# A hybrid decoder layer: the first block's products interleaved with its transposes, and other PSUM banks and places for small work in the dense stage

## The reference

```
u = rmsnorm(h, norm_mix_g);  proj = u @ w_in            # 2824 columns: q, k, v, z, conv inputs, dt
oa = banded attention, window 128, with sinks (4 heads)  # per-head RMS norm of q and k
oc = three dilated attentions, windows 128/512/2048 (4 heads), joined by their softmax weights
ob = SSD scan over causal_dwconv(x, B, C), gated by silu(z)
h  = h + concat(oa, ob, oc) @ w_out
h  = h + square(relu(rmsnorm(h, norm_mlp_g) @ w_up)) @ w_down    # d_ff = 4096
```

## Time and profile before

| | |
|---|---|
| median of three runs | 2558.17 us |
| the profiled execution | 2557.03 us, of which its span is 2554.8 us |
| PE busy | 2410.4 us, 94% of the span |
| DVE, ACT, POOL busy | 1234.8, 846.2, 278.7 us |
| mean granted clock of TensorE | 0.98 of full |
| chain that ended last | PE 74%, DVE 6%, ACT 3%; PE core_dense L2299 alone 64% |

### The profile page before, as it was taken

One profiled execution on the slowest core, in us unless ns is written; L12 is line 12 of the kernel. 1 busy time (PEld: TensorE's weight loads), 2 busy tenths in 40 slices (PEclk: granted clock), 3 DMA queues, 4 the chain that ended last, 5 costly groups with the idle time before them and its releaser, 6 DMA issues.

```text
span 2554.8 us, 43225 instructions
## 1 busy us (share of the span) xinstructions
PE 2410.4 (94%) x17509; PEld 1411.2 (55%) x17509; DVE 1234.8 (48%) x2843; ACT 846.2 (33%) x1533; POOL 278.7 (11%) x305
## 2 busy tenths in 40 slices
PE   7899968999888999999899999989999999999999
PEld 4455535555434555444455554445655447788887
DVE  3445446566646767742644654135566521422222
ACT  4444235464435443331433331124432111311210
POOL 0111222111102211001110100011101001000000
PEclk8899989999999999999999999999999999999999
DMA  6454264665574667775434556533455553322232
GB/s 209 166 173 165 100 229 150 215 209 181 177 237 154 213 204 230 246 257 180 154 118 153 153 163 178 159 119 106 156 172 167 159 163 117 96 92 99 93 99 81
DMA packets 327588, 414.44 MB, mean 162 GB/s; under 512 B 62111, under 2 KB 248095, under 8 KB 327136
## 3 DMA queue, kind: packets, MB, share of 16 engines
q1 hardware_dynamic: 327392, 411.69, 50.0%
HBM read 300.00 MB, written 111.62 MB: 161 GB/s over the span
## 4 chain that ended last, share of the span: by engine, by line
PE 74%; DVE 6%; ACT 3%; issue 2%; DMA 1%; SPq 1%; POOL 0%; DVEq 0%; ACTq 0%; POOLq 0%
PE core_dense L2299 64%; PE core_spare L2399 2%; PE core_spare L2413 1%; PE core_spare L2387 1%; PE core_spare L2425 1%; PE core_spare L2553 1%; DVE core_col L2013 1%; DVE core_p L1939 1%; ACT core_p L1715 1%; PE core_spare L2547 1%; PE core_spare L2531 0%; PE core_spare L2539 0%; DVE core_h L1907 0%; PE core_spare L2533 0%; DVE core_r L1895 0%
## 5 line engine op out<-in xcount | busy, mean ns | idle before, releaser
L2299 PE MATMUL core_dense<-core_u,core_ring 128*128 128x512 f16 (+2 forms) x4800 | 870.2, 342 | 22.2 <-ACT core_yt L1688 5.7
L2299 PEld LDWEIGHTS core_dense<-core_u,core_ring 128*128 128x128 f16 x4800 | 469.4, 98 | 396.4 <-issue 41.0
L2299 PE MATMUL core_dense<-core_r_hi,core_ring 128*128 128x512 f16 (+2 forms) x2560 | 649.0, 339 | 2.7 <-DVE core_h L1907 1.5
L2299 PE MATMUL core_dense<-core_r_lo,core_ring 128*128 128x512 f16 (+2 forms) x1280 | 434.0, 339 | 0.0
L2299 PEld LDWEIGHTS core_dense<-core_r_hi,core_ring 128*128 128x128 f16 x2560 | 250.4, 98 | 197.9 <-issue 5.7
L2299 PE MATMUL core_dense<-tok_u,core_ring 128*128 128x512 f16 x1152 | 266.0, 387 | 16.8 <-DMA core_ring<-scratch_kept_w 16.8
L1680 ACT ACTIVATE core_r<-core_dense 128x512 f32<-128x512 f32 (+2 forms) x160 | 82.3, 515 | 528.9 <-PE core_dense L2299 528.9
L1895 DVE TENSOR_TENSOR core_r<-core_r 128x512 f32<-128x512 f32 (+2 forms) x160 | 96.4, 603 | 321.6 <-ACT core_r L1680 321.2
L628 PE MATMUL tok_prod<-tok_w_hi,tok_u 128*128 128x512 f16 (+1 forms) x768 | 200.4, 351 | 0.0
L2299 PEld LDWEIGHTS core_dense<-tok_u,core_ring 128*128 128x128 f16 x1152 | 114.0, 100 | 147.7 <-DMA core_ring<-scratch_kept_w 14.3
L2299 PEld LDWEIGHTS core_dense<-core_r_lo,core_ring 128*128 128x128 f16 x1280 | 125.2, 98 | 93.4 <-issue 0.7
(11 more groups left out here) (309 smaller groups left out, 2704.3 us busy)
## 6 DMA issues: line engine op xcount, KB each, us to landing
core_ring<-scratch_kept_w SPq DMA_DIRECT2D x264, 512.0 KB, 4.3
scratch_kept_w<-core_ring SPq DMA_DIRECT2D x72, 512.0 KB, 5.6
core_qkv<-out_tok SPq DMA_DIRECT2D x48, 384.0 KB, 5.6
core_staged<-in_w_up SPq DMA_DIRECT2D x32, 512.0 KB, 4.7
core_staged<-in_w_down SPq DMA_DIRECT2D x32, 512.0 KB, 4.6
out_tok<-tok_tok SPq DMA_DIRECT2D x16, 644.0 KB, 3.0
core_piece<-in_c_kt SPq DMA_DIRECT2D x32, 288.0 KB, 3.9
core_piece<-in_c_v SPq DMA_DIRECT2D x16, 576.0 KB, 4.6
```

Of the source, the lines that this page charges most:

```text
L2299: ins = pe.matmul(bank, w[:, k, part, :], s, start=first and j == 0, stop=last and j == 2, skip_group_check=True)
```

## The change

In the tokens stage's first block, the eight `line` copies are all DVE's, so ACT has none ahead of its squares. The first piece of the weights is split before the factors are spread. The products of piece k - 1 come right behind the transposes of piece k, and each weight piece is split in its step. In all blocks, ACT copies the transposes of piece k out before it rounds piece k - 1 (`high`).

In the core, `y`, `tail` and `sum` leave the two dense banks for spare banks 4 and 5, and 2 and 3. The attention slots of blocks 1, 2 and 3 begin 1, 1 and 3 entries later. An `sk` unit stands ahead of the attention slot of its entry, and uses banks 0 and 1 while attention goes on and 3 and 4 after it (before: 4 and 5). The `sx` units are in entries 0, 1, 2 (before: 0, 2, 4), and the `sv` units three entries later.

```diff
     yield "rms", 0, 0, 0
+    yield "w", 0, 0, 0
     yield "spread", 0, 0, 0
-    for k in range(KT):
-        yield "turn", 0, k, 0
-        if k % 2:
-            yield "w", 0, k // 2, 0
-    for k in range(4, KT):
-        yield "w", 0, k, 0
-    yield "pair", 0, 0, 0
+    for k in range(KT + 1):
+        if k < KT:
+            yield "turn", 0, k, 0
+        if 0 < k < KT:
+            yield "w", 0, k, 0
+        if k:
+            yield "pair", 0, k - 1, 0
...
-        take_bank(("line", j), line_act if j % 2 else line_dve)
-    elif kind == "pair":
+        take_bank(("line", j), line_act if j >= 8 and j % 2 else line_dve)
...
+            for kk in (k - 1, k)[0 if k else 1:2 if k == KT - 1 else 1]:
+                high(n, kk)
+
+        def high(n, k):
+            i = turn_no[n, k]
+            w = BLOCKS[n][1] * BLOCKS[n][2]
...
-        def pair():
-            for k in range(KT):
-                pe.wait_ge(ul_ready, turn_no[0, k] + 1)
-                pe.wait_ge(wl_ready, k + 1)
-                for t in range(2):
-                    for q in range(3):
-                        if k == 0:
-                            free(pe, "prod", 0, t, q)
-                        last = thrice(order["prod", 0, t, q][0], 0, t, k, q)
-                        if k == KT - 1:
-                            last.then_inc(prod_done, 1)
+        def pair(k):
+            pe.wait_ge(ul_ready, turn_no[0, k] + 1)
+            pe.wait_ge(wl_ready, k + 1)
...
+HOST_FROM = (1, 1, 3)
...
-            some = [[s] for s in att_slots(att_end[b + 1], att_end[b + 2])]
+            some = [[] for _ in range(HOST_FROM[b])] + [[s] for s in att_slots(att_end[b + 1], att_end[b + 2])]
...
-                    some[5 + 3 * k] = some[5 + 3 * k] + [("sk", k // 2, k % 2, 0)]
+                    some[5 + 3 * k] = [("sk", k // 2, k % 2, 0)] + some[5 + 3 * k]
             if b == 2:
                 for k in range(3):
-                    some[2 * k] = some[2 * k] + [("sx", k, 0, 0)]
+                    some[k] = some[k] + [("sx", k, 0, 0)]
                 for k in range(16):
-                    some[8 + 2 * k] = some[8 + 2 * k] + [("split", 16 + k, 0, 0)]
-                    some[9 + 2 * k] = some[9 + 2 * k] + [("sv", k // 2, k % 2, 0)]
-                some[41] = some[41] + [("se", 0, 0, 0)]
+                    some[11 + 2 * k] = some[11 + 2 * k] + [("split", 16 + k, 0, 0)]
+                    some[12 + 2 * k] = some[12 + 2 * k] + [("sv", k // 2, k % 2, 0)]
+                some[44] = some[44] + [("se", 0, 0, 0)]
             beside = iter(some)
...
+def sk_bank(n, j, s):
+    return (0 if 5 + 3 * (2 * n + j) < att_end[2 + 1] - att_end[2] + 4 else 3) + s
...
-            bank = counts["dense"] % NDENSE
-            bank_of[kind, b, i, q] = dense[bank]
...
+            if kind in ("y", "tail", "sum"):
+                bank = 2 + q if kind == "sum" else 4 + i % 2
+                bank_of[kind, b, i, q] = spare[bank]
+                claim((kind, b, i, q), bank, *free)
+            else:
+                bank = counts["dense"] % NDENSE
+                bank_of[kind, b, i, q] = dense[bank]
+                counts["dense"] += 1
+                claim((kind, b, i, q), f"dense{bank}", *free)
...
-        for bank in (4, 5):
-            claim(("SK", b, i), bank, smp_taken, 2 * b + i + 1)
+        for s in range(2):
+            claim(("SK", b, i), sk_bank(b, i, s), smp_taken, 2 * b + i + 1)```

Three places show what moved. The first is PE in the tokens stage's first block: `tok_turned` are the transposes, `tok_prod<-tok_w_hi,tok_u` the products. Before, from the lines on:

```order
L667 MATMUL tok_prod<-tok_hot,tok_table 128x384 x8
L618 MATMUL tok_turned<-tok_ident,tok_rr 128x128 x4
L610 MATMUL tok_turned<-tok_ident,tok_x 128x128 x32
L628 MATMUL tok_prod<-tok_w_hi,tok_u 128x512 x2
L628 MATMUL tok_prod<-tok_w_lo,tok_u 128x512
```

More of the change, by code:

```diff
@@ L211, in tokens @@
             if kind == "line":
-                take_bank(("line", j), line_act if j % 2 else line_dve)
-            elif kind == "pair":
+                take_bank(("line", j), line_act if j >= 8 and j % 2 else line_dve)
+            elif kind == "pair" and j == 0:
                 for t in range(2):
@@ L300, in store_line @@
                 def store_line(kind):
-                    sp.wait_ge(line_dve, 2 * kind + 2)
-                    sp.wait_ge(line_act, 2 * kind + 2)
+                    sp.wait_ge(line_dve, 4 * (kind + 1) if kind < 2 else 2 * kind + 6)
+                    if kind >= 2:
+                        sp.wait_ge(line_act, 2 * kind - 2)
                     sp.dma_start(io["lines"][kind * 4:kind * 4 + 4, :, :].rearrange("h p l -> p h l"), line[:, kind % 2, :, :]).then_inc(lines_out, 16)
@@ L464, in _ @@
                 for kind, n, j, q in units:
-                    if kind == "line" and j % 2:
+                    if kind == "line" and j >= 8 and j % 2:
                         act.wait_ge(line_done, j + 1)
@@ L477, in _ @@
                         split_w(j)
-                    elif kind == "pair":
+                    elif kind == "pair" and j == KT - 1:
                         for t in range(2):
@@ L568, in _ @@
                 for kind, n, j, q in units:
-                    if kind == "line" and j % 2 == 0:
+                    if kind == "line" and (j < 8 or j % 2 == 0):
                         dve.wait_ge(line_done, j + 1)
@@ L629, in thrice @@
                     return last
-                def pair():
-                    for k in range(KT):
-                        pe.wait_ge(ul_ready, turn_no[0, k] + 1)
-                        pe.wait_ge(wl_ready, k + 1)
-                        for t in range(2):
-                            for q in range(3):
-                                if k == 0:
-                                    free(pe, "prod", 0, t, q)
-                                last = thrice(order["prod", 0, t, q][0], 0, t, k, q)
-                                if k == KT - 1:
-                                    last.then_inc(prod_done, 1)
+                def pair(k):
+                    pe.wait_ge(ul_ready, turn_no[0, k] + 1)
+                    pe.wait_ge(wl_ready, k + 1)
+                    for t in range(2):
+                        for q in range(3):
+                            if k == 0:
+                                free(pe, "prod", 0, t, q)
+                            last = thrice(order["prod", 0, t, q][0], 0, t, k, q)
+                            if k == KT - 1:
+                                last.then_inc(prod_done, 1)
                 def one(n, j, q):
@@ L675, in _ @@
                     elif kind == "pair":
-                        pair()
+                        pair(j)
                     elif kind == "prod":
@@ L1065, in core @@
                     order[kind, b, i, q] = counts[kind]
-                    bank = counts["dense"] % NDENSE
-                    bank_of[kind, b, i, q] = dense[bank]
                     counts[kind] += 1
-                    counts["dense"] += 1
                     if kind in ("y", "tail"):
@@ L1074, in core @@
                         free = ({"out": out_added, "sum": total_log, "up": r_ready, "down": down_added}[kind], counts[kind])
-                    claim((kind, b, i, q), f"dense{bank}", *free)
+                    if kind in ("y", "tail", "sum"):
[7 more added lines that the diff above has]
+                        claim((kind, b, i, q), f"dense{bank}", *free)
                 if kind in ("out", "up", "down"):
@@ L2573, in sampled @@
                                     at = 12 + DEC_T * q
-                                    both(spare[5 - s][:, at:at + DEC_T], lambda l: halves[rows, l, KC * P:], lambda l: qs[rows, l, q, DEC_T * n:DEC_T * n + DEC_T])
+                                    both(spare[sk_bank(n, j, s)][:, at:at + DEC_T], lambda l: halves[rows, l, KC * P:], lambda l: qs[rows, l, q, DEC_T * n:DEC_T * n + DEC_T])
                         for k in range(KC):
@@ L2581, in sampled @@
                                 q0 = DEC_T * n + t0
-                                last = both(spare[5 - s][:, at:at + w], lambda l: halves[rows, l, k * P:(k + 1) * P], lambda l: qs[rows, l, 2 + j, q0:q0 + w])
+                                last = both(spare[sk_bank(n, j, s)][:, at:at + w], lambda l: halves[rows, l, k * P:(k + 1) * P], lambda l: qs[rows, l, 2 + j, q0:q0 + w])
                         last.then_inc(smp_done, 1)
```

5 lines of the change are left out of this document (3 added, 2 removed).

## The result

| | before | after |
|---|---|---|
| median | 2558.49 us (4 runs, 2557.70 to 2562.37) | 2514.47 us (4 runs, 2512.73 to 2516.70) |
| ratio | | 0.9825, 95% interval 0.9808 to 0.9842 |
| the profiled execution, its span | 2557.03, 2554.8 us | 2512.73, 2510.7 us |

The change saves 44 us. The sign and most mechanisms were right; the sum was 20 us short. Of all executions behind the medians of this text one was slow, 4945.12 us of tok_old_core_new, where its other four took 2514.18 to 2517.40.

The account below looks back on a forecast made before the run. PE was taken as busy nearly throughout, so only its idle and half-clock stretches could give time. Terms +9.5 - 10.8 - 3.5 - 14.8 - 4.6 = -24.2 us gave 2534, own range 2527 to 2541, wider range 2521 to 2550.

Parts of the forecast that it names:

- the delay carries on to the end: Tokens stage behind the first block: dense on PE, so the first block's delay stays; ACT's new order there gives 0.
- the signs by which the prediction would have called itself wrong: First-block gaps under 1.5 us, block ending before 66 us, or attention's transposes or scores waiting behind `sk`.
- Part 1: Tokens stage, first block: ACT loses four line copies, so the spread starts at 14.1, not 20.05, 5.95 us earlier.
- Part 2: First block, products between transposes: seven gaps of 2.2 us, four clock drops at 1.7; with part 1 +9.5, range +2.7 to +30.
- the late weight: First block: last weight piece, loaded behind the last `xs` store, comes 3.2 us late at full clock, nothing at half.
- Part 3: Core, `y` and `sum` off the dense banks: waits for DVE's additions go (7.8), 3 of 5.7 at `y`'s copy; -10.8.
- Parts 4 and 6: Core: attention one entry later, second slot finds bank 0 free, -3.5; `sx` in entries 0, 1, 2, -4.6.
- Part 5: Core, `sk` ahead of the slot: waits of 11.0 and half clock worth 5.8 go, new waits 2; -14.8.
- half clock throughout: Rival: first block at half clock throughout, +29.7 in place of 9.5, time 2554; chance 0.08.
- a slower `sk`: Rival, block 1: each of six slots waits for DVE's copies and the clock falls; net +5, 2563; chance 0.05.
- the core's waits come back: Rival: the core's waits return elsewhere, parts 3 to 6 give 20 in place of 33.7, time 2548; chance 0.15.
- the first block keeping its clock: Rival: first block +2.7, time 2527; with a `y` term of -13.5, 2524; chance 0.2.

Follow-up runs that it names:

- tok_old_core_new: The tokens stage of the kernel before with the core of the change; median 2515.77 us, ratio 0.9832.
- squares_only: The kernel before with one edit, the first eight bias lines' copies all on DVE; median 2551.31 us, ratio 0.9971.
- y_on_dense: The kernel after, but `y`, `tail` and `sum` back on the two dense banks; median 2530.95 us, ratio 0.9895.
- sk_behind: The kernel after, but each `sk` unit behind its entry's attention slot, on its old banks; median 2529.94 us, ratio 0.9901.
- two_behind: The kernel after, but the first block's products two pieces behind the transposes, not one; median 2496.20 us, ratio 0.9750.

## Why the prediction was wrong, by its own steps

The failed step is the sentence "All later blocks: ACT's order of copy and rounding changes too. Their steps lie beside products that don't need them: 0", and with it "the delay carries on to the end". That a copy lies beside products is true only as long as what follows it is not late. The trace of before showed that it was: behind the pair PE waited 10.4 us at `z` products and 3.6 at transposes for ACT's copy, and was at half clock from 78.8, 106.1 and 232.4. None of this is in the prediction, whose rows of the tokens stage are of its first block. The stretch got 11.7 us shorter, and the two runs on that edit alone show 9.3 and 10.3.

The 20 us are made up so: 11.7 in the later blocks, 4.7 in the first block and 5.8 in the core came out better than forecast, less 2.2 that the rest up to block 0 took more with the same code. Of the signs by which the prediction would have called itself wrong, two stayed out and the third came at a small size: the gaps were 2.08 us, the pair ended behind 66 us, and of what stands behind `sk` the scores waited 0.8 us, once.

The terms, one by one:

- Part 1, squares at once: 5.95 forecast, 6.3 by squares_only. Right.
- Part 2: the mechanism was right (2.2 us a gap forecast, 2.08 measured; 2.45 at the first, 20 us for the first products, 19.92). The sum was not: +9.5 against +4.8. The seventh step has no transposes and no gap of that kind, since no `turn` stands between the last two groups of products; the sum counted them there (0.6 + 2.2) and the late weight (3.2) as well. The late weight cost 1.74, since the fourth half-clock stretch had filled the rest of that wait, so 1.5 of its 1.7 was counted twice: where that stretch did not fall, in y_on_dense and sk_behind, the wait was 3.76 and 3.45. The steps were 5.95 in place of 6.03. 2.8 + 1.5 + 0.4 is the difference of 4.7. The four drops at 1.7 are what the trace shows, and that there were four is in part luck: with the same code y_on_dense lost 6 us more.
- The Trainium skill (TensorE: Matmul & The Clock Gate, A second HAM failure mode) says that a PE which idles briefly and often goes back and forth between its clocks and loses throughput by it. The stretches here show that. The prediction's reading of it, that each gap would cost, gives too much: four of seven did. The length of the gap alone does not decide: 2.08 us was followed by half clock at 33.51 and not at 27.55.
- Part 3, `y` and `sum`: -10.8 forecast, 12.7 by the waits of before and after, 16.3 by y_on_dense. Mis-sized: of the 5.7 us at `y`'s copy I took 3, for fear of the wait on `core_u` behind it. All 5.7 went and that wait rose only by 1.8 against before; and 1.0 at `sum` was not counted. The 3.4 us of half clock in y_on_dense are that kernel's own.
- Parts 4 and 6, slots and `sx`: -8.1 forecast, 9.6 measured. Block 0's slot gave nothing (1.75 was forecast), block 1's 3.5 with the clock, and block 2 6.1 where 4.6 was forecast for `sx`.
- Part 5, `sk` ahead: -14.8 forecast, 14.2 measured: right. The new waits, taken at 2, are 0.8.
- The rest of the stage to block 0 took 2.2 us more with the same code.

Of the rivals, half clock throughout and a slower `sk` didn't happen, nor did the core's waits come back. The case nearest to the result, the first block keeping its clock with a larger `y` term (2524), was nearly right on `y` and wrong on the clock.

What would have led nearer: the list of waits that rows 5 give for 295 us on, taken for 66 to 319 us too, and the question, for each copy of ACT, what stands ahead of it in ACT's own queue. With 9 to 12 us for that the forecast would have been 2522 to 2525; the rest is the seventh step's gap, counted beside the late weight, and the core's terms.

## What to carry to other kernels

In an in-order engine, put what an idle consumer needs ahead of what waits for a slower engine: a copy held behind a rounding that waited for DVE cost some 10 us over 250 us of the tokens stage, most of it at other units than the one that waited. When an order is changed for one block and applies to all, read the waits of all of them. When two steps are interleaved, the distance must cover the longest path between engines: one piece behind left six gaps of 2.08 us, two behind left none of them and was 18 us faster.

## What the runs showed of the chip

The same gap on the same code is not followed by the same clock. In the kernel after it fell behind every second gap, from the first (2.45 us) on; in y_on_dense behind others, at 28.8, 42.5, 56.1 and, in the wait for the last weight, 69.8 us. There the first group of products ran at half speed nearly to its end as well, by its own rows, though the clock column of the view reads 1.00 from 20 to 28 us (two_behind has the same at 19.99):

```profile
20.00 1.04 PE L636 MATMUL tok_prod<-tok_w_hi,tok_u 128*128 128x512 f16 x2 [2.08 <-DVE tok_u L515]
...
24.47 1.06 PE L636 MATMUL tok_prod<-tok_w_hi,tok_u 128*128 128x512 f16 x2
...
28.61 0.85 PE L636 MATMUL tok_prod<-tok_w_hi,tok_u 128*128 128x512 f16 x2 [2.08 <-DVE tok_u L515]
```

Two products take 1.04 to 1.06 us there and 0.59 at the full clock. Against the kernel after the step of the first group took 1.0 us longer, the wait for the last weight was 3.76 in place of 1.74 us, and the last group took 2.9 us longer at half clock, so the pair ended at 76.84; over the six kernels with this first block it ended between 70.61 and 76.84. The wait of 2.5 us that the prediction cites as followed by full clock came back in squares_only, at 1298.87, and half clock followed it (1300.9). Block 1 so took 481.1 us there and 477.5 before, with the same instructions.

A stage with many such waits thus moves by 4 to 9 us between kernels that don't differ in it (the projection part, 393.8 to 402.5; from the pair to `z` with the old order, 248.4 to 252.8), while, but for this block 1, the blocks repeated to 0.5 us. One profiled execution of such a stage can't judge an edit of a few us by its time. Its idle time is steadier, as the stretch from the pair to `z` shows.
